# Expert rows added to their tokens by one-hot products on PE during the expert stage, in place of row stores and gathers

## What is computed

```python
logits = ht @ w_router + b_router                  # 512 x 32
top_val, top_idx = lax.top_k(logits, 4)
gate = softmax(top_val)
# each expert e, for the rows (tokens) that chose it:
hc = xb @ w1[e] + b1[e]                            # 1024 -> 2048
glu, lin = min(hc[:, :1024], 7), clip(hc[:, 1024:], -7, 7)
y = (glu * sigmoid(1.702 * glu) * (lin + 1)) @ w2[e] + b2[e]
out[token] += gate * y                             # a sum over the token's 4 experts
x = x + out
return rmsnorm(x, g_final)
```

## Time and profile before

| | before |
|---|---|
| median of 3 runs | 1757.15 us (1756.9 to 1759.78) |
| the profiled execution | 1757.28 us |
| its span, first to last instruction | 1755.2 us |
| PE busy | 1649.7 us (94%) |
| DVE busy | 455.9 us (26%) |
| ACT busy | 380.7 us (22%) |
| POOL busy | 110.2 us (6%) |
| moved by DMA | 502.36 MB, mean 286 GB/s |

### The profile page before, as it was taken

The page is one execution under the profiler, slowest core; times in us unless marked ns, Lnnn a source line. Parts: engine busy times, 40 slices in busy tenths (PEclk is TensorE's granted clock), DMA queues, the critical chain, the costliest instruction groups (busy, mean ns, idle before and its releaser), DMA issues.

```text
span 1755.2 us, 34911 instructions
## 1 busy us (share of the span) xinstructions
PE 1649.7 (94%) x14976; PEld 921.2 (52%) x14976; DVE 455.9 (26%) x857; ACT 380.7 (22%) x597; POOL 110.2 (6%) x189
## 2 busy tenths in 40 slices
PE   7989999999999999999999999889989989989995
PEld 6766887888888767434343434333333333333331
DVE  4354527325645243651010100010010010010006
ACT  5464233434335333000000100000000000000001
POOL 0011300000000010000000000000000000000003
PEclk9999999999999999999999999999999999999998
DMA  6203531234225425799999999999999999999997
GB/s 244 73 24 92 169 99 40 74 101 162 96 87 201 168 97 220 311 387 387 409 408 400 401 407 403 407 411 398 411 410 401 409 409 398 409 410 404 410 415 285
DMA packets 104700, 502.36 MB, mean 286 GB/s; under 512 B 11030, under 2 KB 21174, under 8 KB 55056
## 3 DMA queue, kind: packets, MB, share of 16 engines
q1 hardware_dynamic: 83920, 461.40, 66.6%
q0 software_dynamic: 7968, 26.37, 4.7%
q10 hardware_dynamic: 12672, 12.46, 2.0%
HBM read 485.59 MB, written 14.55 MB: 285 GB/s over the span
## 4 chain that ended last, share of the span: by engine, by line
PE 58%; SPq 28%; DMA 7%; issue 3%; DVE 2%; ACT 1%; POOL 1%; ACTq 0%; POOLq 0%; DVEq 0%
SPq L524 27%; PE ps L2007 12%; PE ps L1690 10%; PE ps L1692 10%; PE ps L1691 10%; PE ps L2031 7%; DMA ring<-in_w_exp_in 5%; PE ps L1786 1%; PE ps L1833 1%; PE ps L1853 1%; PE ps L503 1%; DMA y_main<-moe 1%; DMA ring<-y_main,work 1%; SPq L545 1%; PE ps L1775 1%
## 5 line engine op out<-in xcount | busy, mean ns | idle before, releaser
L2007 PE MATMUL ps<-ring,moe 128*32 128x512 f32 x3104 | 348.2, 595 | 30.1 <-DMA ring<-in_w_exp_in 30.0
L1581 DVE TENSOR_SCALAR moe<-ps 128x768 f32<-128x768 f32 (+1 forms) x32 | 26.7, 833 | 858.6 <-PE ps L2007 858.6
L2007 PEld LDWEIGHTS ps<-ring,moe 128*32 128x32 f32 x3104 | 91.1, 110 | 270.8 <-issue 196.1
L1119 DVE TENSOR_TENSOR wl<-raw,wh 128x1024 fp32r<-128x1024 f32 x102 | 123.6, 1224 | 231.7 <-ACT wh L764 231.7
L2031 PE MATMUL ps<-ring,moe 128*32 128x256 f32 x3136 | 174.4, 379 | 1.7 <-DMA ring<-in_w_exp_out 1.7
L764 ACT ACTIVATE wh<-raw 128x1024 fp32r<-128x1024 f32 x102 | 106.9, 1060 | 224.1 <-PE ps L1692 224.1
L1690 PE MATMUL ps<-oph,wh 128*128 128x512 f32 x384 | 151.3, 394 | 4.4 <-DVE opl L1154 2.0
L1016 ACT ACTIVATE moe<-ps 128x768 f32<-128x768 f32 (+1 forms) x32 | 22.7, 710 | 589.7 <-DVE moe L1581 589.7
L1691 PE MATMUL ps<-opl,wh 128*128 128x512 f32 x384 | 150.2, 391 | 0.0
L1692 PE MATMUL ps<-oph,wl 128*128 128x512 f32 x384 | 150.1, 391 | 0.0
L2031 PEld LDWEIGHTS ps<-ring,moe 128*32 128x32 f32 x3136 | 93.7, 110 | 73.2 <-DMA ring<-in_w_exp_out 4.3
(11 more groups left out here) (327 smaller groups left out, 1753.5 us busy)
## 6 DMA issues: line engine op xcount, KB each, us to landing
ring<-in_w_exp_in SPq DMA_DIRECT2D x152, 1024.0 KB, 28.9
ring<-in_w_exp_out SPq DMA_DIRECT2D x78, 1024.0 KB, 28.9
moe<-in_w_exp_in SPq DMA_DIRECT2D x52, 1024.0 KB, 28.7
work<-in_w_exp_in SPq DMA_DIRECT2D x52, 1024.0 KB, 29.1
moe<-in_w_exp_out SPq DMA_DIRECT2D x26, 1024.0 KB, 28.7
raw<-in_w_in SPq DMA_DIRECT2D x25, 1024.0 KB, 5.2
work<-in_w_exp_out SPq DMA_DIRECT2D x24, 1024.0 KB, 28.6
raw<-in_w_ckv SPq DMA_DIRECT2D x8, 1024.0 KB, 5.2
```

The costliest lines, as they stand in the source:

```text
L1119: nc.vector.tensor_tensor(half_lo(g), raw[:, g // 2 % RAW, g % 2 * PC:(g % 2 + 1) * PC], half_hi(g), ALU.subtract).then_inc(w_lo, 1)
L1581: nc.vector.tensor_scalar(act_n[:, 0:g], ps[:, 0:g, 256:512].rearrange("p j (n a) -> p j a n", a=2), 1.0 - LIMIT, 1.0 + LIMIT, ALU.max, AL ...
L2007: ins = nc.tensor.matmul(ps[32 * s:32 * s + 32, j, :], xt[:, k, 32 * j:32 * j + 32], w[:, s, :, :], start=False, stop=(k == KT - 1), tile_ ...
```

## The change

No row is stored to DRAM or gathered from it again after the expert. Each expert's result goes to its tokens by products on PE, as soon as it is there:

- down() writes the first two groups as two halves of 512 columns (bank 4), the third as four quarters of 256 columns (bank 5). ACT copies the result to `y_hi` in float32r (`y_keep`), DVE writes the rest of it to `y_lo` (`y_rest`).
- DVE repeats the comparison of choose for expert p - 1 (`pick_again`), and keeps the tokens' gates of this expert in `shares`. PE turns the one-hot matrix (`spots_turn`, within down(p - 1), after its second chunk), ACT copies it to `spots` as float32r.
- During up(p), after chunks 0, 2, 4 and 6, PE multiplies spots with y_hi and y_lo of expert p - 2 for one tile of 128 tokens (`to_tokens`) into banks 4 and 5, and DVE adds the result, times the gate, to res (`add_tile`).
- PE has new waits: for x_keep before each down(), for spots_keep before act_turn, and for the adds.
- The order at the end is up(31), down(30), down(31); down(31) has expert 30's token tiles between its chunks, and expert 31's follow it. SP's order of loads follows.
- y_main, y_over, place_rows, the last gathers, the diagonal products and own_rows are gone.

```diff
+            def pick_again(n, c, e, g, b, table=None):
+                if n is not None:
+                    dve.wait_ge(spots_made, n)
+                table = fill[g] if table is None else table
+                nc.vector.tensor_copy(shares[:, b, :], gate_te[:, :, bass.ds(e, 1)].rearrange("p t o -> p (t o)"))
+                nc.vector.tensor_tensor(picked[:, :, 0:32 * g], table..., slots..., ALU.is_equal).then_inc(picked_ready, 1)
+            def y_rest(n, g):
+                dve.wait_ge(y_kept, n + 1)
+                if g > 2:
+                    nc.vector.tensor_tensor(y_lo[:, 512:768], ps[:, 5, 0:256], y_hi[:, 512:768], ALU.subtract)
+                nc.vector.tensor_tensor(y_lo[:, 0:512], ps[:, 4, :], y_hi[:, 0:512], ALU.subtract).then_inc(y_split, 1)
+            def add_tile(turn, t, b, bank):
+                dve.wait_ge(comb_done, turn + (t + 1))
+                nc.vector.scalar_tensor_tensor(res[:, t, :], ps[:, bank:bank + 2, :]..., shares[:, b, t:t + 1],
+                                               res[:, t, :], ALU.mult, ALU.add).then_inc(comb_used, 1)
...
+            def turn(p, i, g, to_choose=True):
+                add_all((p - 2) * TT, i)
+                swiglu(p, CYCLE[i], p * EC + UPS)
+                dve.wait_ge(x_in, p * 16 + 16)
+                index(p + 2, CYCLE[i])
+                if to_choose:
+                    choose(expert_at(p + 3), CYCLE[1 - i])
+                e = expert_at(p - 1)
+                pick_again(p - 1, e, e, g, 1 - i)
+                y_rest(p - 1, g)
...
+            def spots_turn(n, g):
+                pe.wait_ge(picked_ready, n + 1)
+                for t in range(TT):
+                    for h in range(2):
+                        for j in range(2):
+                            ins = nc.tensor.matmul(ps[64 * h + 32 * j:64 * h + 32 * j + 32, 6, t * P:(t + 1) * P],
+                                                   picked[:, t, 32 * j:32 * j + 32], ident_b, start=True, stop=True,
+                                                   tile_position=(0, 64 * h + 32 * j), skip_group_check=True)
+                    for s in range(4 * (g - 2)):
+                        ins = nc.tensor.matmul(ps[32 * s:32 * s + 32, 7, t * P:(t + 1) * P], picked[:, t, 64:96], ident_b,
+                                               start=True, stop=True, tile_position=(0, 32 * s), skip_group_check=True)
+                ins.then_inc(spots_made, 1)
+            def to_tokens(n, g, t, bank, used, evens=None):
+                if t == 0:
+                    pe.wait_ge(spots_kept, n + 1)
+                    pe.wait_ge(y_split, n + 1)
+                pe.wait_ge(comb_used, used)
+                def quarter(s, y, start, stop):
+                    rows = slice(32 * s, 32 * s + 32)
+                    return nc.tensor.matmul(ps[:, bank + s // 2, s % 2 * 256:s % 2 * 256 + 256], spots[rows, T + t * P:T + t * P + P],
+                                            y[rows, 512:768], start=start, stop=stop, tile_position=(32 * s, 0), skip_group_check=True)
+                if g > 2:
+                    for y in (y_hi, y_lo):
+                        for s in (0, 2):
+                            ins = quarter(s, y, y is y_hi, False)
+                    ins.then_inc(even_done, 1)
+                for y in (y_hi, y_lo):
+                    for h in range(2):
+                        rows = slice(64 * h, 64 * h + 64)
+                        ins = nc.tensor.matmul(ps[:, bank + h, :], spots[rows, t * P:t * P + P], y[rows, 0:512],
+                                               start=(g == 2 and y is y_hi), stop=(g == 2 and y is y_lo), skip_group_check=True)
+                if g > 2:
+                    pe.wait_ge(even_done, evens)
+                    for y in (y_hi, y_lo):
+                        for s in (1, 3):
+                            ins = quarter(s, y, False, y is y_lo)
+                ins.then_inc(comb_done, 1)
...
             def step(p, i, to_index=True):
-                up(p, CYCLE[i], p * 2 + 1)
-                x_turn(p + 1)
+                up(p, CYCLE[i], p * 2 + 1, between=combs(p - 2))
+                if p < NE - 1:
+                    x_turn(p + 1)
                 if to_index:
                     index(p + 2, CYCLE[i])
-                down(p - 1, groups(p - 1), p * 2)
-                act_turn(p, CYCLE[i], p + 2)
+                pe.wait_ge(xt_kept, min(p + 2, NE))
+                down(p - 1, groups(p - 1), p * 2, between={TURN_AT: lambda: spots_turn(p - 1, groups(p - 1))})
+                act_turn(p, CYCLE[i], min(p + 2, NE), p - 1)
```

More of the change, by code:

```diff
@@ L1051, in _ @@
             x_keep(2, CYCLE[0])
-            y_place(0, groups(0), 0, DOWNS, first=True)
+            spots_keep(0, groups(0))
+            y_keep(groups(0), DOWNS)
             act_keep(1, groups(1))
@@ new lines, in _ @@
+            turn(2, 0, groups(1))
+            turn(3, 1, groups(2))
+            with dve.Fori(1, CYCLES - 2) as m:
+                for i in range(2):
+                    turn(m * 2 + (2 + i), i, CYCLE[1 - i])
+            turn(NE - 4, 0, CYCLE[1])
+            turn(NE - 3, 1, CYCLE[0], to_choose=False)
+            for i in range(2):
+                p = NE - 2 + i
+                add_all((p - 2) * TT, i)
+                swiglu(p, CYCLE[i], p * EC + UPS)
+                e = expert_at(p - 1)
+                pick_again(p - 1, e, e, CYCLE[1 - i], 1 - i)
+                y_rest(p - 1, CYCLE[1 - i])
@@ L1987, in chunk_in, with up @@
                 return held(c)
[L1989 removed]
+            def up(n, g, sel, first=False, over=None, between={}):
                 pe.wait_ge(xt_kept, n + 1)
@@ L2110, in _, with evens_of, combs @@
             index(3, CYCLE[1])
-            down(0, groups(0), 2, first=True)
-            act_turn(1, groups(1), 3)
+            pe.wait_ge(ident_ready, 1)
+            pe.wait_ge(xt_kept, 3)
+            down(0, groups(0), 2, first=True, between={TURN_AT: lambda: spots_turn(0, groups(0))})
+            act_turn(1, groups(1), 3, 0)
+            def evens_of(n):
+                return TT * sum(groups(k) > 2 for k in range(n))
+            def combs(n):
+                return {2 * t: lambda t=t: to_tokens(n, groups(n), t, 4, TT * n + t, evens_of(n) + t + 1) for t in range(TT)}
@@ new lines, in step, with last_but_one @@
+                act_turn(p, CYCLE[i], min(p + 2, NE), p - 1)
+            for p in range(2, NE):
+                step(p, p % 2, to_index=p < NE - 2)
+            def last_but_one(*tiles, spots=False):
+                for t in tiles:
+                    to_tokens(NE - 2, CYCLE[0], t, 2 * (t % 2), TT * (NE - 2) + max(t - 1, 0), evens_of(NE - 2) + t + 1)
+                if spots:
+                    spots_turn(NE - 1, CYCLE[1])
+            down(NE - 1, CYCLE[1], 2 * NE, between={0: lambda: last_but_one(0, 1), 1: lambda: last_but_one(2),
+                                                    2: lambda: last_but_one(3, spots=True)})
```

403 lines of the change are left out of this document (105 added, 298 removed).

## The result

| | before | after |
|---|---|---|
| median | 1757.79 us (1756.90 to 1759.78) | 1880.47 us (1878.56 to 1881.27, 4 runs) |
| ratio | | 1.0695, 95% interval 1.0676 to 1.0713 |
| the profiled execution, its span | 1757.28, 1755.2 us | 1880.35, 1878.6 us |
| PE, DVE busy | 94%, 26% | 96%, 33% |
| moved by DMA | 502.36 MB | 483.56 MB |

The forecast of 1885 us was 4.5 us too high. Seven per cent slower, as expected; the small distance hides two errors that nearly cancel, and one rival whose turning point was put in the wrong place.

What follows compares the result with a forecast made beforehand. Bound by PE until about 985 us, then by weights; after the change by PE throughout. 776.2 + 864.0 + 209.3 + 1.0 = 1850.5, down(31) to 1865.4, tail 17.8: span 1883, time 1885 us; range 1845 to 1925 (0.70).

Steps and rivals of the forecast that it cites:

- PE stays the limit to the end, no DMA wait: Expert stage: PE's pair of experts becomes 71.3 us, over the weights' 64.1, so PE limits throughout.
- The wait for xt_kept: PE waits for x_keep ahead of down(): 1.57 us in one step, 1.08 in the other, 2.65 a pair.
- Token tiles: to_tokens() products plus shape changes on PE: 0.82 us a two-group tile, 1.67 a three-group one; inner changes 0.19 each.
- spots_turn(): Turning the one-hots on PE within down(): 48 products at 0.029 us, 1.3 us a pair; by stream alone 0.7.
- The pair's sum: PE's additions per pair of experts: 2.65 + 3.3 + 6.7 + 1.3 = 13.95 us, making 57.36 into 71.3.
- What lies beside it: DVE and ACT work in the expert stage was claimed covered: pick_again by 1.7 us, y_keep and y_rest by 0.6.
- The tail: Behind the last weight product: 2.3 us to the first token tile, 12.0 of DVE work, 3.5 to the end: 17.8.
- Rival A: Expert stage: shape changes nearly free, spots by stream, 8.85 to about 11 us a pair; 1808 to 1840; chance 0.14.
- C: In to_tokens(), float32r row tiles don't run abreast: 5.5 us a pair more, 1973 us; chance 0.04.
- E: The products don't do what is said, the run stays as it is: about 1757 + 0 to 10; chance 0.03.
- Rival D: In to_tokens(), each pass waits for its weight load: 5.8 us a pair more, 1972 us; chance 0.03.
- Rival B: Expert stage stays DMA-bound, PE's addition fitting under 64.1 - 57.36 = 6.7 us a pair: 1721 us; chance 0.06.

## Why the prediction held, step by step

- **PE stays the limit to the end, no DMA wait.** Shown by the waits, the chain and the line above. The pairs are 70.25 us where no fall comes, 71.3 predicted.
- **The wait for xt_kept.** 1.42 and 1.06, so 2.48 us; predicted 1.57 and 1.08. That nothing could fill the hole was true of the work that the change has; moving the wait by two chunks removes it whole, and 50.6 us with it.
- **Token tiles.** Timeline of PE in a two-group step:

```profile
1248.32 0.50 PE L1968 MATMUL ps<-y_hi,spots 64*128 64x512 f32 x2
...
1248.98 3.64 PE L1893 MATMUL ps<-work,moe 128*32 128x512 f32 x32
1252.55 0.50 PE L1968 MATMUL ps<-y_hi,spots 64*128 64x512 f32 x2
```

  Two groups: 0.66 from first to next weight product, and from tile to tile 4.23 us, of which two chunks alone take 3.43: 0.80; predicted 0.82. Three groups: 1.52, and 6.80 from tile to tile (1217.45 to 1224.25) less 5.15 for two chunks: 1.65; predicted 1.67. So 0.14 us a tile lie at the burst's edges, in bf16 as in float32r (4.11 - 3.43 - 0.54), and no run tells what they are. The inner changes are 0.19, as taken from the earlier trace rows, although those rows never show 32 rows against 64. Whether the 0.16 and 0.21 there are made of the same parts is not shown.
- **spots_turn().** Mis-sized, and the largest error of the sum: 16 products in 1241.72 - 1241.49 = 0.23 us and 32 in 1271.70 - 1271.26 = 0.44, so 0.67 a pair for 1.3. The figure "by stream alone", 0.7, was right; the row that I preferred, of bias products, has twice the columns, so half its 0.029 was the better reading of it.
- **The pair's sum.** 2.48 + 4 x 0.80 + 4 x 1.65 + 0.67 = 12.95 us for 13.95; 57.36 + 12.95 = 70.3, and 70.25 was measured.
- **The clock.** Not in the sum. 15 x 1.05 us too much for the pairs, 15.8, stands against 13.6 too little for the falls. Of the 4.6 us too much in the span (1883.2 for 1878.6), up(2) has 0.3 (its weights start at 775.9 for 776.2), and the stretch from there to the end of act_turn(31), 1069.9 us for 1074.3, has 4.4: the pairs' 15.8 less 11.9 for the seven falls that lie in it, and 0.5 more. The forecast was right for its mechanism; that it came within 0.3% is luck, because these two nearly cancel.
- **What lies beside it.** No wait on PE for y_rest, pick_again, spots_keep or the adds between 850 and 1850 us: all the covers held. One sign on the list was missed: PE is busy 96%, not 97% or more, and what is missing is the hole, which the sum contained.
- **The tail.** Predicted 17.8 us behind the last weight product. Timelines of all engines:

```profile
1859.04 1.89 PE L1925 MATMUL ps<-moe 128*32 128x512 f32 x16
...
1863.20 2.48 DVE L1470 SCALAR_TENSOR_TENSOR work<-ps,work 128x1024 f32<-128x1024 f32 x2 [0.87 <-PE ps L1968]
...
1873.78 1.29 DVE L1535 SCALAR_TENSOR_TENSOR work<-work,small 128x1024 f32<-128x1024 f32 x1 [0.27 <-ACT small L1043]
```

  The last chunk's 16 products end their stream at 1859.04 + 1.7, about 1860.8, and the span at 1878.6: 17.8. Its parts are right too: 2.4 to the first add, 11.9 to the end of the last norm, 3.5 behind it, for 2.3, 12.0 and 3.5.
- **Rival A** is out in its main part, free changes, by the run in one shape; its spots by stream was right. C is out by the passes of that run, E by 1721.5 us without the products.
- **Rival D** was half right. Its reading, a load in front of each pass, isn't there: in the one-shape run passes of 0.12 us follow each other with loads of 0.19. But once for each run of passes a price shows that falls from 0.197 to 0.083 us with the load's time, and that is the "change of shape" of the sum. The Trainium skill (TensorE: Matmul & The Clock Gate, Part 3, The mechanism) lets a load overlap only where the row group differs; inside a burst this case's rows speak against it again, since the next load of the same 64 rows is hidden there (0.12 us between passes, 0.19 us a load).
- **Rival B had the wrong threshold.** I wrote that the weights decide at 6.7 us a pair, from which the time falls to 1721. Two errors are in that. First, an addition of 6.7 that only just fits leaves PE the limit from the start, at 64.1 in every pair, and by the line above that is 1769 us, not 1721. Break-even is at 6.1, and 1721 is reached at 3.9 (61.24). Secondly, a pair at 61.24 us runs under the "floor" of 64.1 nearly to the end without PE waiting for weights. I took the floor for a bound on each pair, but the ring's 20 slots of 1 MB are a stock: the change holds PE back from 750 us on, where before emptied the ring at 57.36 us a pair, so at 61.24 us the stock lasts for nearly the whole stage. The bytes show the stock being used: 25.8 MB a pair at 405 GB/s is 63.8 us, so a pair of 61.24 brings 1.0 MB too little, and the window over 13 pairs is 13 MB short, of a ring of 20. After uses and brings the same. That a deeper ring would last longer is not shown; no run changed it.

## What to carry to other kernels

Where one engine paces a stage, time its loop in one pair of rows, price each addition on that engine by the distance of starts in the nearest rows, and ask which wait is only placed too early: here moving one wait by two chunks gave 50.6 us of 122.7. Short bursts of small tiles on PE paid 0.2 us with float32r and 0.08 with bf16 for each run of one tile shape, so keep one shape in a burst (zero rows in place of another shape saved 0.73 and 0.84 us a pair here) and the stationary side in a type that loads fast. A transfer-bound stage with a deep ring has a stock, so compare the whole stage's bytes with its time before calling the mean rate a floor for every step.

## What was not expected of the hardware

- The granted clock can fall to half for some 3.4 us behind an idle hole of 1.4 us on PE, 1.7 us each time. It did so in 6 of 13 pairs of after, in 6 of 13 without the products, in 4 of 13 with another order of the same products, in 3 of 13 with one shape, and never where the hole was filled to 0.4 us or gone. Between 850 and 1700 us the five runs that have the wait ahead of down() unfilled have 67 holes of 1.3 us or more and 25 falls, each behind one of them, and none behind 64 holes of 1.0 us. Why one hole is followed by a fall and the next equal one isn't stays open. So does why the kernel before, whose PE waits for weights up to 1.8 us at a time in the same stretch (1.62 in the earlier trace rows), shows no fall there; a fall does follow its wait of 2.16 us at 1704 us. The same kernel with the wait for x_keep added has eight falls between 900 and 1550 us.
- PE starts products of different row tiles out of the order of the program (both high parts at 1210.9 us, both low ones at 1211.3), so that they run abreast.
- 128 columns of bf16 load in 0.093 us, 128 of float32r in 0.183, and 512 columns stream in 0.23 us either way.
